# A two-block transformer step on one core: where 72 modulation pieces are reduced, and the order of the first block tile of the second feed-forward layer

## The chip, the cores and the metric

The kernel runs on one core of a Trainium2 chip. The metric is device time in microseconds, the median of the runs of one build. Three runs of the kernel before stand at 2033.03, 2033.26 and 2036.62 us.

## The reference, cut to what matters

Two transformer blocks follow each other on a sequence of 512 positions and width 1024, all in 32-bit floats. The first block has three sublayers: a gated feed-forward layer (`ffn1`), a mixer with a short convolution and stick-breaking attention, and a second gated feed-forward layer (`ffn2`). Each sublayer is modulated by vectors that come from a small input `c`:

```python
c_act = jax.nn.silu(c)
mod = (c_act @ w_ada[l] + b_ada[l]).reshape(B, N_SUBLAYERS, N_MOD, D_MODEL)
u = modulate(rmsnorm(h, norm2_g[l]), mod[:, 1, 0], mod[:, 1, 1])
y = mixer(u, ...)
h = h + mod[:, 1, 2][:, None, :] * y
```

The modulation is one row times a 1024 x 9216 matrix of 36 MB. The second block is not touched by the change.

## The kernel before, in words

Features lie on the 128 partitions, positions on the free axis. Weights come in chunks of 128 x 1024 floats (512 KB). Each chunk is loaded by the SyncE queue (SP) into one of four places of `WRAW` (`Weights.load`, L812), rounded by ScalarE into a high part (`Weights.round`, L823, the instruction is L833) and subtracted by VectorE or GpSimd into a low part (`Weights.low`, L847; `low_pool`, L862). TensorE then multiplies in three passes, high by high, high by low and low by high (`mm3`, L988 to L992). A chunk of 8 slices is 24 matmuls over 512 columns. Four places of high and low parts mean that the rounding of chunk c + 3 waits for the end of chunk c - 1.

Each engine's program is written out by hand, in one order, with semaphores between engines. What stands later in an engine's program waits for what stands before it. SP's queue carries both the weight loads and the loads of the modulation.

**Modulation.** It is cut in 72 pieces, each 128 outputs by 1024 inputs (512 KB). SP loads a piece into a place of `ADA` (`sync_modulation`, L3542, the DMA is L3554), and VectorE multiplies and sums it in one instruction (`dve_modulation`, L2417, the instruction is L2432), then reads the accumulator and, for 40 of the pieces, scales the result. The pieces are counted from 0. Pieces 0 to `ADA_FIRST` - 1 are reduced in the first layer and lie in six places under the arrays `TH1` and `UF1` that the layer forms later; the last of them use only four places. The others are reduced in the mixer and lie in four other places (`ADA1`), which are free once `ffn1` has ended. A load waits for the reduction of the piece that its place held (the fourth before) and of the piece six before.

**The mixer's first 14 chunks** are `mix v` 0 to 3, `mix ga` 0 to 6, `mix q` 0, `mix k` 0 and `mix ga` 7. The four `mix v` chunks all accumulate into four PSUM banks, which VectorE drains at L2677 after the last of them (`v_evac`). There are six banks in the ring, so `mix ga` 0 and 1 go to free banks, and `mix ga` 2 needs the first bank that `v_evac` drains. In VectorE's program of the kernel before, each of the four `mix v` steps has the low part of the chunk three further on and then 4, 3, 3 and 3 pieces; then come the four `v_evac`; then seven `mix ga` steps of a low part and two pieces; then the two last pieces after `qk_evac(0, 0)`. SP loads three pieces beside each `mix v` chunk and two beside the others. The first softmax of the attention (`act_mixer`, the activation at L1959 and its wait ahead of it) waits for the last piece, since its tile `T1` lies over the places of `ADA1`.

**The block tiles of `ffn2`.** From hidden tile 3 on the layer multiplies in seven block products a tile instead of eight (`pe_quads`, L1340). In order of TensorE they are m6, m5, m7, then m1 and m2 of the next tile, then m4 and m3. m1, m6, m7 and m4 accumulate in one bank, and ScalarE takes copies of it in between (`snap`, L2065): m7 waits for the copy after m6, and m4 for the copy after m7. Weight sums `sa` and `sb` are formed by VectorE (`dve_first_sums`, `dve_sums`) and rounded and subtracted like chunks. `c22` is VectorE's sum that m3 waits for. `glu` (`dve_glu`, L2492) is the gated product of hidden tiles 0 to 2, which are made without blocks.

Of the kernel before, what the change touches and what calls it, by code (L numbers as in the profile page):

```python
# [14 lines left out]
KD = D // 128  # L15
# [22 lines left out]
    [(v, m) for v in MOD_ORDER[2:] for m in range(KD)]  # L38
NADA = 6

ADA_FIRST = 43


def ada_place(i):

    if i < ADA_FIRST:
        return 0, i % NADA if i < ADA_FIRST - 4 else i % 4
    return 1, i % 4


# [2003 lines left out]
def act_quads(s, name, p, rest=None):  # L2054


    mem, W, on, act = s.mem, s.W, s.on_act, s.act
    fs, B = QUADS[name][p], mem.blocks[name]
    before = QUADS[name][p - 1][-1] if p and QUADS[name][p - 1] else None
    later = [W.at[name, "down", p, m] for m in range(3)]  # L2060
    M1, U1, U2 = mem.TMP[:, 0, 0:256], mem.TMP[:, 0, 256:S], mem.TMP[:, 1, 0:256]

    def snap(x, f, out):
        on.wait_ge(*s.quad(x, name, f))
        act.activation(out, s.P[:, s.bank[name, "m1", f], 0:256], FN.Copy).then_inc(  # L2065
            *s.snap.inc(x, name, f))

    def silu(f):
        x = B.sil[:, f % 2, :]
        on.wait_ge(*s.comb("c12", name, f))  # L2070
        act.activation(x, x, FN.Silu).then_inc(*s.silu.inc(name, f))

    def upper(f):
        on.wait_ge(*s.glu(name, f))
        if p:
            on.wait_ge(*W.done(W.at[name, "down", p - 1, KD - 1]))
        act.activation(B.hi[:, f - PARTS[p][0], :], B.sil[:, f % 2, :], FN.Copy).then_inc(
            *s.a_hi.inc(name, f))

    if before is not None:  # L2080
        on.wait_ge(*s.comb("c11", name, before))
    snap("m1", fs[0], M1)
    if rest:
        rest()
    W.round(W.gate(name, fs[0] + 1))
    for f in fs:
        W.round(W.up(name, f))
        if f != fs[0]:
            silu(f - 1)
        elif before is not None:  # L2090
            on.wait_ge(*s.comb("c12", name, before))
        snap("m6", f, U1)
        if f != fs[0]:
            upper(f - 1)
        elif before is not None:
            on.wait_ge(*s.glu(name, before))
        if f != fs[-1]:
            W.round(("sb", name, f + 1))
            snap("m7", f, U2)
            W.round(("sa", name, f + 1))  # L2100
            on.wait_ge(*s.comb("c11", name, f))
            snap("m1", f + 1, M1)
            W.round(W.gate(name, f + 2) if f + 2 in fs else later[0])
        else:
            snap("m7", f, U2)
            W.round(later[2])
            silu(f)
            upper(f)
# [380 lines left out]
                      OP.mult).then_inc(*s.fgm.inc())  # L2489


def dve_glu(s, name, e, f, hi, lo, SIL):  # L2492
    dve, on = s.dve, s.on_dve
    if e == "gate":
        return
    x, j = SIL[:, f % 2, :], f - PARTS[PART_OF[f]][0]
    on.wait_ge(*s.W.done(s.W.at[name, "up", f]))
    on.wait_ge(*s.silu(name, f))
    dve.tensor_tensor(x, s.psum(name, "up", f), x, OP.mult).then_inc(*s.glu.inc(name, f))
    on.wait_ge(*s.glu(name, f))  # L2500
    on.wait_ge(*s.a_hi(name, f))
    dve.tensor_tensor(lo[:, j, :], x, hi[:, j, :].bitcast(F32), OP.subtract).then_inc(
        *s.a_lo.inc(name, f))
# [11 lines left out]
def dve_first(s):  # L2515
    mem, W, on, dve = s.mem, s.W, s.on_dve, s.dve

    def down(p, m):
        dve_down(s, "ffn1", p, m, GATE1, s.x_in[m // 2]())
        if p == 2:  # L2520
            dve_total(s, "ffn1", m)

    todo = [(e, f) for f in range(PARTS[0][1]) for e in ("gate", "up")]
    prev = None
    for n, (e, f) in enumerate(todo):
        if n < 5:
            if n == 0:
                W.low(6)
            dve_glu(s, "ffn1", e, f, mem.AH1, mem.AL1, mem.SIL1)
            if n == 4:  # L2530
                dve_modulation(s, 1)
            continue
        if prev:
            dve_glu(s, "ffn1", *prev, mem.AH1, mem.AL1, mem.SIL1)
        W.low(W.at["ffn1", e, f] + 3)
        dve_modulation(s, 2)
        prev = e, f
    dve_glu(s, "ffn1", *prev, mem.AH1, mem.AL1, mem.SIL1)
    assert s.next_ada == ADA_FIRST - 4
    for p in range(3):  # L2540
        if p:
            dve_quads(s, "ffn1", p)
        later = act_later("ffn1", p, W)
        for m in range(KD):
            if m:
                down(p, m - 1)
            if p < 2 and m == 6:
                dve_first_sums(s, "ffn1", PARTS[p + 1][0])
                dve_sums(s, "ffn1", PARTS[p + 1][0])
            W.low(W.at["ffn1", "down", p, m + 3] if m < 5 else later[m - 5])  # L2550
            if p == 0 and m < 4:
                dve_modulation(s, 1)

                x = slice(2 * m, 2 * m + 2)
                on.wait_ge(*s.u_lo_p(2 * m + 1))
                on.wait_ge(*s.u_hi("start", 2 * m + 1))
                dve.tensor_tensor(mem.blocks["ffn1"].full[:, x, :], mem.UH[:, x, :].bitcast(F32),
                                  mem.UL[:, x, :].bitcast(F32), OP.add).then_inc(
                                      *s.comb.inc("u full", m))
                if m == 3:  # L2560
                    on.wait_ge(*s.comb("u full", 3))
                    for t in FORMS:
                        dve_form(s, "ffn1", t)
            if p == 0 and m == 4:
                for t in FORMS:
                    dve_form_low(s, "ffn1", t)
        down(p, KD - 1)
    assert s.next_ada == ADA_FIRST

# [99 lines left out]
def dve_mixer(s):  # L2669
    dve, on, mem, W, Z = s.dve, s.on_dve, s.mem, s.W, s.Z  # L2670
# [9 lines left out]
    def qk_evac(w, p):  # L2680
        dve_pairs(s, "a", w, p, mem.Qa, mem.Ka, mem.KLa,
                  s.psum(("mix q", "mix k")[w], p), 0.125 if w == 0 else 1.0)
# [31 lines left out]

    for q in range(4):
        W.low(W.at["mix v", q] + 3)
        dve_modulation(s, 3 if q else 4)
    for tb in range(4):
        v_evac(tb)
    for m in range(KD - 1):  # L2720
# [4 lines left out]
    dve_modulation(s, 2)  # L2725
    W.low(W.at["mix k", 0] + 3)
    qk_evac(1, 0)
    assert s.next_ada == len(PIECES)
    W.low(W.at["mix ga", KD - 1] + 3)
    on.wait_ge(*s.ple_mm(3))  # L2730
    dve.memset(mem.CV[:, 0:2], 0.0).then_inc(*s.cv.inc("pad"))

# [1 line left out]
    c = W.at["mix ga", KD - 1]  # L2734
# [78 lines left out]
def dve_second(s):  # L2813
    mem, W, on, dve = s.mem, s.W, s.on_dve, s.dve
# [11 lines left out]
        dve_total(s, "ffn2", m, 0)  # L2826
        dve_total(s, "ffn2", m, 1)

    def glu(e, f):
        dve_glu(s, "ffn2", e, f, mem.AH2, mem.AL2, mem.SIL2)  # L2830

    def form(t):
        dve_form_low(s, "ffn2", t)
# [15 lines left out]
    glu("up", 1)  # L2849
    W.low(("sb", "ffn2", 3))  # L2850
    W.low(("sa", "ffn2", 3))
    glu("up", 2)
    for p in range(3):
        dve_quads(s, "ffn2", p)
        later = act_later("ffn2", p, W)
# [755 lines left out]
def sync_mixer(s):  # L3611
# [5 lines left out]
    sync_modulation(s, ADA_FIRST + 3)  # L3617
    for c in range(W.at["mix v", 0], W.at["mix ga", KD - 1] + 1):
        W.load(c + 7)
        sync_modulation(s, s.ada_at + (2 if c < W.at["mix ga", 0] else 1))  # L3620
    assert s.ada_at == len(PIECES)

    def gb_out(m):
# [269 lines left out]
```

## Time and profile before

| what | value |
|---|---|
| median of three runs | 2033.26 us |
| the profiled execution, its own time | 2033.56 us |
| its span, first to last instruction | 2032.3 us |
| TensorE busy | 1995.2 us, 98% of the span |
| VectorE busy | 1287.0 us, 63% |
| ScalarE busy | 929.9 us, 46% |
| GpSimd busy | 291.7 us, 14% |
| mean granted TensorE clock | 0.998 |

The table is of one profiled execution. Matmuls are pipelined, so a duration of a matmul (0.39 us for 512 columns) is longer than the distance between two starts; the distance is what a matmul costs. The times of the rows further down count from the first instruction. A row of the timeline gives start, duration, engine, line, operation and tiles, and in brackets the idle time of that engine just before and what ended it.

### The profile page before, as it was taken

To read this page: it belongs to the slowest core of one execution; us is meant where nothing else is said; L and a number is where in the kernel's file an instruction comes from. 1 tells how busy PE (TensorE), PEld (TensorE's weight loads), DVE (VectorE), ACT (ScalarE), POOL (GpSimd) and SP (SyncE) were. 2 spreads that over 40 slices of the span, in tenths; PEclk is the share of its full clock that TensorE was granted. 3 is DMA by queue.
4 is the path that set the end of the run, shared out by engine and by line. 5 is a ranking of instruction groups with operands and counts; after the bars stand their busy time and mean duration, and the time that the engine had idled before them with its cause. 6 is when DMAs were issued, how large, how long until landed. Compare 5 with 4: busy or idle time off the path is not lost.

```text
span 2032.3 us, 27032 instructions
## 1 busy us (share of the span) xinstructions
PE 1995.2 (98%) x10637; PEld 1726.1 (85%) x10637; DVE 1287.0 (63%) x1915; ACT 929.9 (46%) x1356; POOL 291.7 (14%) x219
## 2 busy tenths in 40 slices
PE   6999999989999999999999999999999999999998
PEld 5889999778888889899898888888888888888888
DVE  6888767685565668577576445454376575563666
ACT  4334525425656545345255455554434343342444
POOL 5000000002101200000000344443000021020130
PEclk9999999999999999999999999999999999999999
DMA  8943424692223533323233433333535333333232
GB/s 307 334 140 99 123 79 118 216 339 76 77 83 104 181 99 108 116 84 115 84 106 122 131 119 104 119 102 123 196 106 170 99 109 100 94 99 98 82 113 76
DMA packets 84398, 261.49 MB, mean 129 GB/s; under 512 B 9248, under 2 KB 13472, under 8 KB 84272
## 3 DMA queue, kind: packets, MB, share of 16 engines
q1 hardware_dynamic: 84272, 259.77, 39.8%
q8 instruction: 84, 1.38, 0.3%
q14 instruction: 42, 0.34, 0.1%
HBM read 242.92 MB, written 16.81 MB: 128 GB/s over the span
## 4 chain that ended last, share of the span: by engine, by line
PE 72%; DVE 4%; ACT 3%; issue 1%; DMA 1%; POOL 0%; DVEq 0%; SPq 0%; ACTq 0%
PE P L990 22%; PE P L991 22%; PE P L992 22%; PE P L1225 1%; PE P L1507 1%; DMA ADA<-w_ada 1%; PE P L1237 1%; PE P L1236 1%; ACT WH L833 1%; DVE WL L847 0%; DVE ADA L2432 0%; PE P L1554 0%; DVE SL L2754 0%; DVE TMP L2610 0%; ACT UH L2317 0%
## 5 line engine op out<-in xcount | busy, mean ns | idle before, releaser
L990 PE MATMUL P<-UH,WH 128*128 128x512 f32 (+1 forms) x1563 | 581.5, 372 | 11.8 <-DVE V L2677 5.2
L991 PE MATMUL P<-UL,WH 128*128 128x512 f32 (+1 forms) x1563 | 577.1, 369 | 0.0
L992 PE MATMUL P<-UH,WL 128*128 128x512 f32 (+1 forms) x1563 | 577.1, 369 | 0.0
L833 ACT ACTIVATE WH<-WRAW 128x1024 fp32r<-128x1024 f32 (+2 forms) x311 | 311.2, 1011 | 437.5 <-PE P L992 433.9
L847 DVE TENSOR_TENSOR WL<-WRAW,WH 128x1024 fp32r<-128x1024 f32 (+2 forms) x252 | 303.1, 1206 | 76.7 <-ACT WH L833 76.1
L990 PEld LDWEIGHTS P<-UH,WH 128*128 128x128 f32 x1563 | 295.9, 189 | 61.8 <-issue 10.9
L992 PEld LDWEIGHTS P<-UH,WL 128*128 128x128 f32 x1563 | 295.8, 189 | 49.9
L991 PEld LDWEIGHTS P<-UL,WH 128*128 128x128 f32 x1563 | 296.1, 189 | 47.3
L862 POOL TENSOR_TENSOR WL<-WRAW,WH 128x1024 fp32r<-128x1024 f32 x59 | 144.7, 2454 | 356.8 <-ACT WH L833 356.8
L990 PE MATMUL P<-AH,WH 128*128 128x512 f32 x478 | 186.6, 390 | 0.0
L991 PE MATMUL P<-AL,WH 128*128 128x512 f32 x478 | 186.1, 389 | 0.0
L992 PE MATMUL P<-AH,WL 128*128 128x512 f32 x478 | 186.0, 389 | 0.0
L992 PEld LDWEIGHTS P<-AH,WL 128*128 128x128 f32 x478 | 89.7, 188 | 18.8
L990 PEld LDWEIGHTS P<-AH,WH 128*128 128x128 f32 x478 | 89.8, 188 | 18.6 <-POOL AL L3510 0.4
L991 PEld LDWEIGHTS P<-AL,WH 128*128 128x128 f32 x478 | 89.8, 188 | 18.1
L990 PE MATMUL P<-TH,WH 128*128 128x256 f32 x352 | 99.7, 283 | 0.7 <-ACT TMP L2065 0.7
L992 PE MATMUL P<-TH,WL 128*128 128x256 f32 x352 | 99.6, 283 | 0.0
L991 PE MATMUL P<-TL,WH 128*128 128x256 f32 x352 | 99.6, 283 | 0.0
L3401 POOL TENSOR_TENSOR R<-VAR,NEGHALF 128x4 f32<-128x4 f32 (+1 forms) x9 | 10.4, 1157 | 607.7 <-DVE VAR L2982 362.7
L2432 DVE CUSTOM_DVE_ANT_0 ADA<-ADA,CB,COLS 128x1024 f32<-128x1024 f32 x56 | 75.4, 1352 | 8.3 <-DMA ADA<-w_ada 8.2
L2511 DVE SCALAR_TENSOR_TENSOR H<-P,MOD,H 128x512 f32<-128x512 f32 x48 | 35.9, 748 | 67.7 <-PE P L992 67.7
L3278 DVE SCALAR_TENSOR_TENSOR Y<-ZP,COLS,Y 128x512 f32<-128x512 f32 x88 | 69.1, 785 | 14.5 <-ACT Y L2296 12.8
(347 smaller groups left out, 3564.9 us busy)
## 6 DMA issues: line engine op xcount, KB each, us to landing
WRAW<-w_gu SPq DMA_DIRECT2D x88, 512.0 KB, 3.6
ADA<-w_ada SPq DMA_DIRECT2D x72, 512.0 KB, 5.9
WRAW<-w_down SPq DMA_DIRECT2D x48, 512.0 KB, 3.6
WRAW<-w_up SPq DMA_DIRECT2D x44, 512.0 KB, 3.6
WRAW<-w_in SPq DMA_DIRECT2D x40, 512.0 KB, 3.6
WRAW<-w_mix SPq DMA_DIRECT2D x36, 512.0 KB, 3.6
WRAW<-w_down SPq DMA_DIRECT2D x24, 384.0 KB, 3.1
WRAW<-w_out SPq DMA_DIRECT2D x16, 512.0 KB, 4.1
```

Source lines behind the costliest of these rows:

```text
L833: s.act.activation(hi, self.raw(item), FN.Copy).then_inc(*self.rounded.inc(item))
L847: s.dve.tensor_tensor(lo, self.raw(item), hi.bitcast(F32), OP.subtract).then_inc(*self.low_v.inc(item))
L862: s.pool.tensor_tensor(lo, self.raw(item), hi.bitcast(F32), OP.subtract).then_inc(*self.low_p.inc(item))
L990: pe.matmul(out, wh, xh, start=start, stop=False, skip_group_check=True)
L991: pe.matmul(out, wh, xl, start=False, stop=False, skip_group_check=True)
L992: return pe.matmul(out, wl, xh, start=False, stop=stop, skip_group_check=True)
L1225: s.pe.matmul(out, x, y, start=start and i == 0, stop=False, skip_group_check=True)
L1236: pe.matmul(ob[:, 128 * j:S], v, hi[:, of], start=j == 0, stop=False, skip_group_check=True)
L1237: last = pe.matmul(ob[:, 128 * j:S], v, lo[:, of], start=False, stop=j == 3, skip_group_check=True)
L2432: dve.tensor_tensor_reduce(piece, piece, c, 1.0, s.col("b_ada", v * KD + m), OP.mult, OP.add, mod).then_inc(*s.ada.inc(i, "sum"))
L2511: s.dve.scalar_tensor_tensor(h, s.psum(name, "down", p, m), s.mod(gate, m), h, OP.mult, OP.add).then_inc(*s.resid.inc(name, p, m))
L3278: dve.scalar_tensor_tensor(y, mem.ZP[:, n % 3, j:S + j], s.col("conv_w_2", 2 * NF * j + i), y, OP.mult, OP.add).then_inc(*s.conv.inc(e, f, j))
```

## The change

Four edits go together for the modulation. `ADA_FIRST` goes from 43 to 44, so one more piece is reduced in `ffn1`, in the step of the first `down` chunk (two pieces there, one in each of the next three). In the mixer VectorE reduces two pieces in each of fourteen steps: the four `mix v` steps, the seven `mix ga` steps, and after `qk_evac(0, 0)`, after `qk_evac(1, 0)` and after the low part three chunks past `mix ga` 7. That is 8 + 14 + 2 + 2 + 2 = 28. SP loads two pieces beside each chunk instead of three beside the first four. Its four pieces ahead of the first stay.

In `ffn2`, ScalarE rounds the gate chunk of hidden tile 4 before it makes the high part of `glu` 2 instead of after it, and VectorE subtracts that chunk's low part between the product of `glu` 2 and its low part. In the first block tile (hidden tile 3) the copies after m7 and after m1 of the next tile go ahead of the rounding of both weight sums.

```diff
-ADA_FIRST = 43
+ADA_FIRST = 44
@@ ada_place
-        return 0, i % NADA if i < ADA_FIRST - 4 else i % 4
+        return 0, i % NADA if i < ADA_FIRST - 5 else i % 4
@@ act_quads
     snap("m1", fs[0], M1)
+    W.round(W.gate(name, fs[0] + 1))
     if rest:
         rest()
-    W.round(W.gate(name, fs[0] + 1))
...
         if f != fs[-1]:
-            W.round(("sb", name, f + 1))
-            snap("m7", f, U2)
-            W.round(("sa", name, f + 1))
-            on.wait_ge(*s.comb("c11", name, f))
-            snap("m1", f + 1, M1)
+            if rest and f == fs[0]:
+                snap("m7", f, U2)
+                on.wait_ge(*s.comb("c11", name, f))
+                snap("m1", f + 1, M1)
+                W.round(("sa", name, f + 1))
+            else:
+                W.round(("sb", name, f + 1))
+                snap("m7", f, U2)
+                W.round(("sa", name, f + 1))
+                on.wait_ge(*s.comb("c11", name, f))
+                snap("m1", f + 1, M1)
@@ dve_glu
     dve.tensor_tensor(x, s.psum(name, "up", f), x, OP.mult).then_inc(*s.glu.inc(name, f))
+    if rest:
+        rest()
@@ dve_first
-                dve_modulation(s, 1)
+                dve_modulation(s, 1 if m else 2)
@@ dve_mixer
     for q in range(4):
         W.low(W.at["mix v", q] + 3)
-        dve_modulation(s, 3 if q else 4)
+        dve_modulation(s, 2)
...
     W.low(W.at["mix k", 0] + 3)
     qk_evac(1, 0)
+    dve_modulation(s, 2)
+    W.low(W.at["mix ga", KD - 1] + 3)
+    dve_modulation(s, 2)
     assert s.next_ada == len(PIECES)
-    W.low(W.at["mix ga", KD - 1] + 3)
@@ dve_second
-    glu("up", 2)
+    glu("up", 2, lambda: W.low(W.gate("ffn2", 4)))
@@ sync_mixer
         W.load(c + 7)
-        sync_modulation(s, s.ada_at + (2 if c < W.at["mix ga", 0] else 1))
+        sync_modulation(s, s.ada_at + 1)
```

`W.round(("sa", ...))` works through the list of preparations up to its item, and `sb` stands before `sa` in it, so both are rounded there.

## Rows read from the trace of the kernel before

**Rows 1.** Waits of TensorE: total us, times, longest.
```profile
PE P L990 <- DVE V L2677: 5.2, 1, 5.2
PE P L990 <- DVE WL L847: 1.2, 1, 1.2
```

**Rows 2.** Busy time by window: us, then each engine, clock, DMA share, GB/s.
```profile
400.00:405.00 5.00, 3.94 (x18) 2.94 (x16) 3.68 (x7) 0.96 (x1) 0.00 (x0) 1.00 1.03 411
...
421.50:425.00 3.50, 3.40 (x8) 2.75 (x9) 3.50 (x5) 0.00 (x0) 0.00 (x0) 0.51 0.63 249
```

**Rows 3.** Timeline of ScalarE, the roundings that wait for a chunk's end.
```profile
404.04 1.06 ACT L833 ACTIVATE WH<-WRAW 128x1024 fp32r<-128x1024 f32 x1 [4.10 <-PE P L992]
410.97 1.06 ACT L833 ACTIVATE WH<-WRAW 128x1024 fp32r<-128x1024 f32 x1 [3.92 <-PE P L992]
...
429.00 1.06 ACT L833 ACTIVATE WH<-WRAW 128x1024 fp32r<-128x1024 f32 x1 [10.91 <-PE P L992]
...
434.44 1.06 ACT L833 ACTIVATE WH<-WRAW 128x1024 fp32r<-128x1024 f32 x1 [3.80 <-PE P L992]
```

**Rows 4.** Timeline of VectorE from the first mixer piece to the V drain.
```profile
397.44 1.29 DVE L2432 CUSTOM_DVE_ANT_0 ADA<-ADA,CB,COLS 128x1024 f32<-128x1024 f32 x1 [3.53 <-DMA ADA<-w_ada]
...
401.37 1.29 DVE L2432 CUSTOM_DVE_ANT_0 ADA<-ADA,CB,COLS 128x1024 f32<-128x1024 f32 x1 [1.32 <-DMA ADA<-w_ada]
...
403.86 1.22 DVE L847 TENSOR_TENSOR WL<-WRAW,WH 128x1024 fp32r<-128x1024 f32 x1
...
410.50 1.28 DVE L2432 CUSTOM_DVE_ANT_0 ADA<-ADA,CB,COLS 128x1024 f32<-128x1024 f32 x1
...
415.25 1.22 DVE L847 TENSOR_TENSOR WL<-WRAW,WH 128x1024 fp32r<-128x1024 f32 x1
...
420.77 2.48 DVE L2677 TENSOR_TENSOR V<-P,V 128x512 fp32r<-128x512 f32 x4
```

**Rows 5.** Timeline of SP, the first mixer pieces issued.
```profile
393.60 1.80 SPq L3554 DMA_DIRECT2D ADA<-w_ada  x4
...
398.77 4.26 SPq L3554 DMA_DIRECT2D ADA<-w_ada  x3
```

**Rows 6.** Tile ADA, 393 to 465 us.
```profile
DMA to landing us min/median/max: 3.8/5.8/7.7
```

**Rows 7.** Timelines of VectorE and ScalarE, head 0.
```profile
465.17 1.39 DVE L2651 TENSOR_TENSOR aKL<-P,aK 64x512 fp32r<-64x512 f32 x2 [1.34 <-ACT aK L1854]
...
476.87 2.08 DVE L2754 TENSOR_TENSOR SL<-T,SH 128x1280 fp32r<-128x1280 f32 x1 [1.52 <-ACT SH L1966]
...
469.99 1.23 ACT L1959 ACTIVATE T<-P 128x1280 f32<-128x1280 f32 x1
```

**Rows 8.** Chain of waits, TensorE's first use of the softmax.
```profile
484.85 1.23 PE P L1294 x8
```

**Rows 9.** Timeline of TensorE, first block tile of `ffn2`.
```profile
786.67 0.28 PE L991 MATMUL P<-TL,XH 128*128 128x256 f32 x1
786.79 0.28 PE L992 MATMUL P<-TH,XL 128*128 128x256 f32 x1
787.42 0.39 PE L990 MATMUL P<-TH,XH 128*128 128x256 f32 x1 [0.35 <-ACT TMP L2065]
...
792.73 0.39 PE L990 MATMUL P<-TH,WH 128*128 128x256 f32 x1 [0.73 <-ACT TMP L2065]
```

**Rows 10.** Timelines of ScalarE and VectorE, the same tile.
```profile
785.53 1.05 ACT L833 ACTIVATE XH<-WRAW 128x1024 fp32r<-128x1024 f32 x1
...
791.34 1.06 ACT L833 ACTIVATE WH<-SB 128x1024 fp32r<-128x1024 f32 x1 [3.98 <-DVE SB L2894]
...
793.58 0.42 DVE L2919 TENSOR_TENSOR TMP<-P,TMP 128x256 f32<-128x256 f32 x1
```

**Rows 11.** Timelines of VectorE and TensorE, before `ffn1`'s first block tile.
```profile
140.97 4.62 DVE L2585 TENSOR_TENSOR TL<-UF,TH 128x1024 fp32r<-128x1024 f32 x4
...
156.50 0.28 PE L990 MATMUL P<-UH,WXH 128*128 128x256 f32 x1
```

More of the change, by code:

```diff
@@ L2489, in dve_start, with dve_glu @@
                       OP.mult).then_inc(*s.fgm.inc())
-def dve_glu(s, name, e, f, hi, lo, SIL):
+def dve_glu(s, name, e, f, hi, lo, SIL, rest=None):
     dve, on = s.dve, s.on_dve
@@ L2538, in dve_first @@
     dve_glu(s, "ffn1", *prev, mem.AH1, mem.AL1, mem.SIL1)
-    assert s.next_ada == ADA_FIRST - 4
+    assert s.next_ada == ADA_FIRST - 5
     for p in range(3):
@@ L2827, in down, with glu @@
         dve_total(s, "ffn2", m, 1)
-    def glu(e, f):
-        dve_glu(s, "ffn2", e, f, mem.AH2, mem.AL2, mem.SIL2)
+    def glu(e, f, rest=None):
+        dve_glu(s, "ffn2", e, f, mem.AH2, mem.AL2, mem.SIL2, rest)
     def form(t):
```

## The prediction

> **What bounds the kernel now.** The first view to read is the waits of TensorE, since that engine is busy 98% of the span and has only a handful of idle places left. Two of them lie in the mixer's first chunks and both name VectorE [rows 1]: 5.2 us before `mix ga` 2, which waits for the V drain, and 1.2 us before `mix ga` 0, which waits for its low part. VectorE is busy 63% over the whole span, so its mean says nothing here. Its own timeline does [rows 4]: the low part of `mix ga` 0 stands behind four pieces and starts at 403.86, and the V drain stands behind thirteen pieces and starts at 420.77. The pieces in turn came late because SP could issue the first only at 393.60 [rows 5] and the DMA engines were full from 400 on, at 411 GB/s [rows 2]. So this stretch is bounded by loading and reducing pieces ahead of two things that TensorE needs, while the places where the pieces are needed themselves are far away.
>
> The second view is the window after the gap: in 421.5 to 425 the granted clock is 0.51, the lower of its two levels (1.2 instead of 2.4 GHz), right after TensorE had stood still for over 5 us; in the windows before it it is 1.00 [rows 2]. The gap costs twice.
>
> What both cost together is read from ScalarE, whose roundings start as a chunk ends [rows 3]. Undisturbed, 429.00 to 434.44 is 5.44 us a chunk. The end of `mix v` 3 is at 404.04, those of `mix ga` 0 and 2 at 410.97 and 429.00.
>
> **The mixer, what can be won.** From 404.04 to 429.00 are 24.96 us for three chunks, which at 5.44 need 16.32. Lost: 24.96 - 16.32 = 8.64 us. It splits as 6.93 - 5.44 = 1.49 for the low part and 18.03 - 10.88 = 7.15 for the V drain with the slow clock. The ceiling of this part is 8.6 us; by TensorE's own starts the idle stretches and half of the slow window of 3.5 us [rows 2] come to a little less, so I take 8.5.
>
> **The mixer, replayed.** A piece costs VectorE 1.28 us [rows 4], or 1.45 with its scaling as I take it, a low part 1.15 to 1.22. TensorE ends `mix v` 3 at about 403.8, and then wants `mix ga` 0 at 403.8, `mix ga` 1 at 409.2, `mix ga` 2 at 414.7.
> - Step 0 has two pieces. They land as now, so they run from 397.44 to about 400.0. The low part of `mix ga` 0 follows and ends at 401.3, where it now starts at 403.86. Wanted at 403.8: 2.5 us to spare, the gap of 1.2 goes.
> - Step 1: the third piece can start at 401.37, as now, when it lands [rows 4]; the two end at 403.9, the low part of `mix ga` 1 at 405.1. Wanted at 409.2.
> - Step 2: these pieces are issued when the first two places come free, at 398.77 [rows 5] and about 400.1. With the median of 5.8 us to landing [rows 6] they are there at 404.6 and 405.9; reduced by 407.8, and the low part of `mix ga` 2 ends at 409.0, where it now starts at 415.25. Wanted at 414.7.
> - Step 3: issued at about 402.6 and 403.9, landed at 408.4 and 409.7, or with the longest landing of 7.7 us [rows 6] the last at 411.6. Reduced by 411.8 (412.9 at the longest). The V drain starts then; TensorE started 421.60 - 420.77 = 0.83 us after the drain's start [rows 4, 1], so the bank is free at 412.7 (413.8). Wanted at 414.7: 2.0 us to spare (0.9).
>
> A check from the other side, without any thought on the DMA: even if nothing landed earlier than now, the eighth piece starts at 410.50 [rows 4]. One low part more ahead of it makes that 411.7, the piece ends at 413.0 and the bank is free at 413.9, still before 414.7. So the gap before `mix ga` 2 goes whole and so does the slow clock behind it. The bounds of this part are 8.6 us won, and 3.9 us won if the last piece came 3 us too late and the clock fell again (8.6 - 3.0 - 1.7); I take 8.5, since both replays end there.
>
> After that a step of VectorE is two pieces and a low part, 2.6 to 2.9 + 1.2 = 3.8 to 4.1 us, in a chunk of 5.44. Loads: three times 524 KB in 5.44 us is 289 GB/s, against the 411 seen [rows 2]. Nothing builds up.
>
> On that the Trainium skill, "DMA: Bandwidth & Descriptors", section "Where 436 GB/s comes from", speaks against me: it says that loads from HBM are held to about 358 GB/s for a core. The trace exceeds it, with 411 over 5 us [rows 2]. By 411 the eleven transfers up to the eighth piece (5.77 MB) take 14.0 us, by 358 they take 16.1; as an estimate from that page, the rule would take 2.1 us of step 3's spare time, leave nothing of it, and by it the rival of a rest of the gap would be about twice as likely as I put it below.
>
> **What is moved, and who waits for it.** (a) Pieces at the tail. VectorE now does its last four pieces, in two pairs, after `qk_evac(1, 0)`, which ends at 466.6 now [rows 7] and at 458.1 when all is 8.5 us earlier. Four pieces with scaling, 4 x 1.39 = 5.6 us, end at about 463.6. The first softmax activation, now at 469.99 [rows 7], would start at 461.5 and waits 2.1 us for the last piece. Behind it in ScalarE's program stand the rest of head 0's softmax and the roundings. TensorE fills with three chunks and wants the result at 484.69 to 484.85 [rows 8]; VectorE delivers it at 476.87 + 2.08 = 478.95 [rows 7]. Of 5.7 us spare 2.1 are used. Cost 0; if the cover were gone it would be the 2.1. (b) SP: fewer pieces stand ahead of the weight loads in the first steps, so these go out earlier; at the tail the load behind the last two pieces waits for a low part that comes after their places are free. Cost 0: a load is issued for the chunk seven further on, 38 us at 5.44 a chunk. (c) The piece in `ffn1` costs VectorE 1.3 us in the first `down` step, and its load holds the next weight load by about 1.5 us. The forms behind it end at 140.97 + 4.62 = 145.6, and TensorE's first block matmul is at 156.50 [rows 11]: 10.9 us spare. Cost 0, and at most 0 gained, as TensorE isn't idle there.
>
> **The block tile.** Matmuls over 256 columns start 0.12 us apart (786.67, 786.79). 786.79 to 787.42 is 0.63, so 0.51 is lost before m7; before m4 the same reading of the idle 0.73 gives 0.90 [rows 9]. Ceiling 1.41. The copy that m7 waits for stands behind the rounding of the gate chunk at 785.53 [rows 10], 0.95 us at ScalarE's pace; moved into ScalarE's idle time before the `glu` product, it lets the copy run at 786.05, before m5 has ended at 786.9. The first 0.51 goes. The copy that m4 waits for stands behind the rounding of `sb`, which waits 3.98 us for VectorE's sum [rows 10]; ahead of it, it runs at about 788.5, and m4 starts when m2 ends, at 791.3. The next late thing is `c22`, which m3 waits for: it stands in VectorE's program behind the low part of `sb`, and its rounding starts with the sum, 1.1 us earlier than now because VectorE's work moved up by that. `c22`, now 793.58 to 794.0 [rows 10], ends at 792.9, and m3 is wanted at 792.7. So 0.25 stays: 1.15 won. Bounds: 1.41 won, and 0.74 lost, if `sb` were late for m6 by the two copies (0.37 each) now ahead of it. I take 1.15, as m6 of tile 4 is wanted at 794.5 and the low part is there at 792.5.
>
> **Sum.** 8.5 + 1.15 = 9.65 us. Between 830 and 1970 us TensorE never waits, and the head gaps of the mixer hang on chains that move with it, so nothing takes it back. The profiled execution took 2033.56, 1.26 more than its span; it becomes 2023.9. The median is 0.3 lower: 2033.26 - 9.65 = 2023.6.
>
> **Rivals.**
> - A rest of the gap stays before `mix ga` 2, because the extra weight loads now share the DMA engines with the pieces. For it: 411 GB/s is all that they gave [rows 2], and a landing of 7.7 us has been seen [rows 6]. Against it: the check above. At 3 us of idle time and a slow clock after it, 8.5 - 4.7 + 1.15 = 4.95 won: 2028.3. Chance 0.10.
> - The block tile gives nothing, `c22` or `sb` taking the place of the copies: 2033.26 - 8.5 = 2024.8; at its worst bound 2025.5. For it: VectorE is all but busy there. Chance 0.10.
> - The gain is given back later in the mixer, no change: 2033. Against it: no idle time of TensorE outside the head gaps. Chance 0.04.
> - Slower: the last piece holds head 0. Place: the first softmax activation, its price one for one in TensorE from the point where the last piece ends 3.6 us after 463.6, that is after 467.2. To be slower than before it must end after 467.2 + 9.65 = 476.9; at 481 the time would be 2037.4. For it: the two last pieces are issued only when the pair before the last is reduced, behind a weight load that waits for GpSimd. Against it: they are issued at about 453 and land by 461 even at 7.7 us. Chance 0.02.
> - The forecast: 0.74.
>
> **How the numbers follow.** The likeliest is 2023.6, with its own range of 2022.4 to 2025. The range for 8 in 10 takes in the second rival and the mild form of the first: 2021.5 to 2026.8. A measurement of this kernel tells about 0.2%, 4.1 us, from no change. Faster by more: 0.74 + 0.10 + 0.10 less a little for a first rival in its worst form, 0.93. Within it 0.05, slower 0.02.
>
> **What would show it.** No wait of TensorE at the V drain and none at `mix ga` 0's low part; roundings of ScalarE from 404.04 on every 5.44 us; clock 1.00 through 425; the V drain starting between 411 and 414; the first softmax activation waiting for a piece by about 2 us and TensorE not waiting at L1294 in head 0; in `ffn2` m7 without a wait and at most 0.3 us left at m3. Wrong would be: a V drain after 414.7, or a wait of TensorE in head 0 that is not in the list now.

## The result and the profile after

The changed kernel takes 2023.26 us, the median of four runs (2023.12 to 2023.8), beside 2033.28 for the kernel before (2033.03 to 2036.62, four runs). The ratio is 0.9947, with a 95% interval of 0.993 to 0.9965: 0.35 to 0.7% faster. The median fell by 10.0 us, forecast were 9.65. The profiled execution took 2023.12, with a span of 2021.9 and a mean granted clock of 0.998.

The waits of TensorE after, where those of [rows 1] stood; columns: engine, tile, line, released by, total us, times, longest:

```profile
PE P L1303 <- DVE RL L2775: 2.7, 4, 0.8
PE P L1294 <- DVE SL L2765: 0.7, 2, 0.3
PE P L990 <- DVE TMP L2930: 0.2, 1, 0.2
```

Neither the V drain nor the low part of `mix ga` 0 is in the list any more. Of `ffn2`'s first block tile 0.2 is left, at m3. The first two lines are head gaps of the mixer, which were there before.

Busy time by window after (us, then each engine, granted clock, DMA share, GB/s). The first window is the full load of [rows 2] seen about two microseconds earlier, the others are the places of the gap and of the lower clock:

```profile
398.00:403.00 5.00, 5.00 (x24) 4.14 (x23) 3.93 (x6) 0.90 (x2) 0.00 (x0) 1.00 1.03 410
416.40:421.50 5.10, 5.10 (x24) 4.24 (x23) 4.99 (x11) 1.64 (x2) 0.00 (x0) 1.00 0.93 304
421.50:425.00 3.50, 3.50 (x17) 2.88 (x16) 3.46 (x7) 0.26 (x1) 0.00 (x0) 1.00 0.92 303
```

TensorE is busy in all of it, and from 421.5 to 425 it is granted 1.00 where it had 0.51. ScalarE's roundings, which start as a chunk ends, answer to [rows 3]:

```profile
402.98 1.06 ACT L833 ACTIVATE WH<-WRAW 128x1024 fp32r<-128x1024 f32 x1 [4.10 <-PE P L992]
408.42 1.06 ACT L833 ACTIVATE WH<-WRAW 128x1024 fp32r<-128x1024 f32 x1 [2.44 <-PE P L992]
413.86 1.06 ACT L833 ACTIVATE WH<-WRAW 128x1024 fp32r<-128x1024 f32 x1 [2.37 <-PE P L992]
419.30 1.06 ACT L833 ACTIVATE WH<-WRAW 128x1024 fp32r<-128x1024 f32 x1 [3.80 <-PE P L992]
```

Three chunks take 419.30 - 402.98 = 16.32 us, to the hundredth the undisturbed pace, where they took 24.96.

VectorE after, from the first mixer piece to the V drain, answers to [rows 4]:

```profile
396.38 1.28 DVE L2438 CUSTOM_DVE_ANT_0 ADA<-ADA,CB,COLS 128x1024 f32<-128x1024 f32 x1 [3.51 <-DMA ADA<-w_ada]
...
399.07 1.28 DVE L2438 CUSTOM_DVE_ANT_0 ADA<-ADA,CB,COLS 128x1024 f32<-128x1024 f32 x1 [1.40 <-DMA ADA<-w_ada]
400.28 1.22 DVE L847 TENSOR_TENSOR WL<-WRAW,WH 128x1024 fp32r<-128x1024 f32 x1
...
410.45 1.27 DVE L2438 CUSTOM_DVE_ANT_0 ADA<-ADA,CB,COLS 128x1024 f32<-128x1024 f32 x1
411.90 2.47 DVE L2686 TENSOR_TENSOR V<-P,V 128x512 fp32r<-128x512 f32 x4
```

The low part of `mix ga` 0 now starts at 400.28 (before at 403.86), the V drain at 411.90 (before at 420.77).

Where the 10.44 us between the two profiled executions lie (2033.56 - 2023.12):

| stretch | before | after | difference |
|---|---|---|---|
| span's start to the start of `mix v` 0 | 381.90 | 380.87 | -1.0 |
| from there to head 0's scores | 84.92 | 76.25 | -8.7 |
| `ffn2`, first block tile, 97 starts of matmuls | 13.11 | 11.97 | -1.1 |
| everything else | | | +0.4 |

The third row counts from the first to the last of 97 starts of matmuls. That is 96 distances, and without a stop they take 96 x 0.12 = 11.52 us.

The first row is not the change's work: TensorE's granted clock comes up for good at 29.0 us in the one execution and at 26.7 in the other, and in the twelve further traces at 24.7 to 29.2. Of the last row 0.5 stands at the very end: the clock falls to its lower level 8.6 us before the span's end, 6.5 before.

### The profile page after: what moved, and what is told of

Its sections match the earlier page's. It is cut to its first block, busy times and chain, and to the rows that moved or that the text cites. A ratio compares the mean times of both kernels' runs of the same rounds, so it can differ in the third digit from the quotient of the medians.

```text
span 2021.9 us, 27033 instructions
## 1 busy us (share of the span) xinstructions
PE 1992.1 (99%) x10637; PEld 1724.7 (85%) x10637; DVE 1283.2 (63%) x1915; ACT 930.0 (46%) x1356; POOL 292.2 (14%) x219
## 4 chain that ended last, share of the span: by engine, by line
PE 93%; DVE 3%; ACT 3%; issue 1%; DMA 0%; POOL 0%; SPq 0%; DVEq 0%; ACTq 0%; POOLq 0%
PE P L990 29%; PE P L992 29%; PE P L991 29%; PE P L1225 1%; PE P L1507 1%; PE P L1237 1%; PE P L1236 1%; ACT WH L833 0%; PE P L1103 0%; DVE SQ L2419 0%; PE P L1554 0%; DVE WL L847 0%; DVE SL L2765 0%; DMA H<-x 0%; ACT UH L2323 0%
## 5 line engine op out<-in xcount | busy, mean ns | idle before, releaser
L833 ACT ACTIVATE WH<-WRAW 128x1024 fp32r<-128x1024 f32 (+2 forms) x311 | 311.2, 1011 | 424.1 <-PE P L992 420.4
L3412 POOL TENSOR_TENSOR R<-VAR,NEGHALF 128x4 f32<-128x4 f32 (+1 forms) x9 | 10.4, 1157 | 605.8 <-DVE VAR L2993 361.6
L3289 DVE SCALAR_TENSOR_TENSOR Y<-ZP,COLS,Y 128x512 f32<-128x512 f32 x88 | 69.1, 785 | 14.5 <-ACT Y L2302 12.8
```

The source lines that it names most:

```text
L833: s.act.activation(hi, self.raw(item), FN.Copy).then_inc(*self.rounded.inc(item))
L3289: dve.scalar_tensor_tensor(y, mem.ZP[:, n % 3, j:S + j], s.col("conv_w_2", 2 * NF * j + i), y, OP.mult, OP.add).then_inc(*s.conv.inc(e, f, j))
```

## The experiments

Each line of a diff is against the changed kernel. The differences are taken against the kernel before in the same comparison; its median was 2033.7 to 2034.6 there.

### The parts alone

The mixer's and first layer's part alone; all edits in `ffn2` undone (`act_quads` goes back to its old order as well):

```
-    glu("up", 2, lambda: W.low(W.gate("ffn2", 4)))
+    glu("up", 2)
```

> The modulation's part of the change alone; the block tile of ffn2 stays as before. Theory (the two parts add up, each where the prediction put it): TensorE has no wait at the V drain or at mix ga 0's low part, the two waits of 0.35 and 0.73 us in ffn2's first block tile are back, and the time is 1.1 us over the changed kernel's 2023.3: 2024.4, some 8.8 below before. Rival (the mixer gives less than its 8.6 and the rest of the 10.0 came from the start of the run, where the clock rose 2.3 us earlier in the one trace): that part stays a matter of each run, and the medians would give 7.5 to 8.2 below before, 2025.1 to 2025.8.

Measured: 2024.47 us (2024.05 to 2026.18), ratio 0.9954 (0.9942 to 0.9967), 9.7 us faster where I had 8.8: the time is the expected one, the kernel before was slower in this comparison. The stretch from `mix v` 0 to the scores is 76.26 long, as in the changed kernel, and the two waits of [rows 9] are back, 0.35 and 0.73, with 13.11 us for the 97 starts.

The tile alone; the modulation's spread undone, with the last two pairs at the end taken out, the other counts and SP's as before:

```
-ADA_FIRST = 44
+ADA_FIRST = 43
-        dve_modulation(s, 2)
+        dve_modulation(s, 3 if q else 4)
```

> The order of ffn2's first block tile alone; the modulation as before. Theory: 1.15 us off the path, 2032.1, both waits of TensorE at the copies gone and 0.2 to 0.3 us at m3 in their place. Rival (the copies' waits are only moved on, c22 or sb taking their place): no wait less in sum, 2033.2. The gaps of 1.2 and 5.2 us in the mixer stay as they were in either case.

Measured: 2032.71 us (2030.54 to 2034.8), ratio 0.9994 (0.9985 to 1.0003), 1.5 us faster by the medians; the interval holds no change. By the trace the tile is 11.97 long, as in the changed kernel. Its wait at the V drain, and the window behind it:

```profile
PE P L990 <- DVE V L2686: 6.1, 1, 6.1
```
```profile
421.50:427.00 5.50, 5.50 (x14) 4.30 (x15) 5.50 (x9) 0.00 (x0) 0.00 (x0) 0.53 0.71 249
```

The same program of modulation as before, yet a gap of 6.1 instead of 5.2, and behind it TensorE works 5.3 us at the lower clock instead of 3.4. So this stretch isn't the same in every execution. That fits how far apart the runs lie: those of the kernel before 3.6 to 5.1 us in each comparison (2030.9 to 2035.7 here), those of the changed kernel, where the stretch is gone, 0.7, though the mixer's part alone, without the gap as well, has 2.1. The parts add up: 9.7 + 1.1 by the trace are 10.8, and the changed kernel's 2023.3 lies 10.9 below this comparison's 2034.2.

### Inside the mixer's part

SP's loads as before, three pieces for each step of `mix v`:

```
-        sync_modulation(s, s.ada_at + 1)
+        sync_modulation(s, s.ada_at + (2 if c < W.at["mix ga", 0] else 1))
```

> The changed kernel, but SP loads three pieces beside each mix v chunk as before, so that only VectorE's order is new. Theory (what freed TensorE is VectorE's order, not thinner loading): 2023.3, no wait at the V drain; weight loads go out behind one piece more each, with a lead of seven chunks that is not used up. Rival (three pieces and a weight in 5.44 us, 386 GB/s, fill the DMA engines, so the pieces that count come later): the V drain starts 1.5 to 3 us later than in the changed kernel and TensorE waits 0.5 to 2 us before mix ga 2: 2024 to 2027.

Measured: 2023.34 us (2022.72 to 2023.81), ratio 0.9946 (0.9933 to 0.996). The V drain starts at 410.1, 1.8 earlier than in the changed kernel's trace, and buys nothing, for there TensorE didn't wait. Nor is the 1.8 the work of these loads: the next run has the changed kernel's loads up to the drain, and there it starts at 410.0. SP's edit by itself is worth nothing here.

One piece less in the first layer, three at the very end, and SP issues one more beside `mix ga` 0:

```
-ADA_FIRST = 44
+ADA_FIRST = 43
-                dve_modulation(s, 1 if m else 2)
+                dve_modulation(s, 1)
-    dve_modulation(s, 2)
+    dve_modulation(s, 3)      # the last of the three calls
```

> The changed kernel with ADA_FIRST 43 again: the 29th piece is reduced at the very end, three after mix ga 7's low part. Theory (the 44th piece in ffn1 only keeps the tail short, and the tail has spare time): the first softmax activation waits about 1.4 us longer for the last piece than in the changed kernel (3.5 instead of 2.1), TensorE still doesn't wait in head 0, 2023.3. Rival (the tail is on the path): 1.4 us more, 2024.7.

Measured: 2023.02 us (2022.31 to 2023.84), ratio 0.9945 (0.9931 to 0.9958). The first softmax activation, by ScalarE's timeline (in brackets what it waited and for whom):

```profile
463.38 1.24 ACT L1959 ACTIVATE T<-P 128x1280 f32<-128x1280 f32 x1 [3.44 <-DVE MOD L2438]
```

It waits 3.44 us, and TensorE none: that wait has cover. The 44th piece in the first layer costs and brings nothing.

Eight pieces at the tail, none beside the last two `mix ga` steps of the loop:

```
-        dve_modulation(s, 2)
+        dve_modulation(s, 2 if m < 5 else 0)
...
-    dve_modulation(s, 2)
+    dve_modulation(s, 4)      # both of the last two calls
```

> The changed kernel with no pieces in the steps of mix ga 5 and 6, and four instead of two in each of the last two places, so that eight pieces stand behind qk_evac(1, 0). Theory (head 0 has 3.9 us to spare in the changed kernel, 471.07 to 474.91): there are four places, so the fifth to eighth of the tail can be loaded only as the first four are reduced, 5 to 6 us each from issue to landing; the last ends 7.5 us later than now, the first softmax activation waits some 9.5 us, and TensorE waits 2 to 4.5 us at L1294 in head 0: 2025.3 to 2028. This is the mechanism of the slower rival of the prediction, forced. Rival (head 0 has fill enough, the softmax is not near the path): no wait, 2023.2.

Measured: 2029.79 us (2029.01 to 2030.84), ratio 0.9979 (0.997 to 0.9989). TensorE's waits, ScalarE's timeline, and the window behind the wait:

```profile
PE P L1294 <- DVE SL L2765: 4.7, 3, 4.1
```
```profile
470.43 1.25 ACT L1959 ACTIVATE T<-P 128x1280 f32<-128x1280 f32 x1 [10.22 <-DVE MOD L2438]
```
```profile
479.00:484.00 5.00, 4.94 (x17) 4.56 (x18) 3.71 (x7) 4.14 (x6) 1.47 (x1) 0.50 0.25 92
```

The place of the slower rival is real: where the activation waits 10.22 us, 4.1 reach TensorE, within my 2 to 4.5. But the clock is at 0.50 for 6.8 us, from 477.4 on. TensorE starts again at 479.1 and works the last 5.2 of them at half speed, of which half, 2.6, is lost as well. 4.1 + 2.6 = 6.7 explains the excess over the changed kernel, 6.5; without the clock my 2025.3 to 2028 was too low.

### How thick the pieces may stand

Three pieces in the first two steps, two in the last two, one pair less at the end:

```
-        dve_modulation(s, 2)
+        dve_modulation(s, 3 if q < 2 else 2)
```

> The changed kernel with 3, 3, 2 and 2 pieces in VectorE's four mix v steps instead of 2 each; the last pair of the tail goes instead. Theory (the replay: each piece ahead of the V drain is 1.4 us, and the drain has about 1 us to spare at TensorE): in the changed kernel's trace the drain starts 8.9 us after mix v 3's end, in others of its kind 7.5; two pieces more make 11.7 or 10.3, with 0.83 to the first matmul 12.5 or 11.1, against the 10.88 of two chunks. TensorE waits 0.2 to 1.7 us before mix ga 2 and the clock stays up: 2023.5 to 2025. Rival (loading and not VectorE's queue sets the drain, e3's loads showing that there is room): the two pieces hide in waits and nothing is lost, 2023.2.

Measured: 2032.46 us (2030.67 to 2035.0), ratio 0.9993 (0.9983 to 1.0002). Missed: I had 2023.5 to 2025, and nothing of the mixer's gain is left. TensorE's waits:

```profile
PE P L990 <- DVE V L2686: 3.8, 1, 3.8
...
PE P L1225 <- DVE aKL L2660: 1.7, 1, 1.7
```

Three pieces in all four steps, two pairs less at the end:

```
-        dve_modulation(s, 2)
+        dve_modulation(s, 3)
```

> The same with 3 pieces in each of the four mix v steps, 12 ahead of the drain (13 in the kernel before, 8 in the changed one). Theory: four pieces more are 5.6 us, so the drain starts 13.1 to 14.5 us after mix v 3's end and TensorE waits 3.0 to 4.5 us before mix ga 2; the low part of mix ga 0 behind three pieces comes 0 to 0.3 us late. If the clock falls after it as it did after 5.2 us, 1.7 to 3.4 us more: 2026.3 to 2027.9 without, 2028 to 2031 with. Rival (the gain came from thinner loading in the four steps): SP loads as in the changed kernel, so no more than 1 us is lost.

Measured: 2060.8 us (2060.15 to 2062.44), ratio 1.0131 (1.0115 to 1.0148): 27 us slower than before, far outside what I expected. Its waits:

```profile
PE P L990 <- DVE V L2686: 12.1, 1, 12.1
PE P L1225 <- DVE aKL L2660: 9.3, 1, 9.3
PE P L990 <- DVE WL L847: 7.7, 4, 3.1
```

My replays had counted VectorE's work and the DMA engines' rate. Neither is full here: VectorE waits 43.6 us for pieces, in 16 places. VectorE's timeline and SP's queue in the same stretch:

```profile
426.50 1.22 DVE L847 TENSOR_TENSOR WL<-WRAW,WH 128x1024 fp32r<-128x1024 f32 x1
...
432.61 1.28 DVE L2438 CUSTOM_DVE_ANT_0 ADA<-ADA,CB,COLS 128x1024 f32<-128x1024 f32 x1 [4.90 <-DMA ADA<-w_ada]
```
```profile
427.74 0.33 SPq L821 DMA_DIRECT2D WRAW<-w_mix  x1
428.11 0.91 SPq L3563 DMA_DIRECT2D ADA<-w_ada  x2
```

The low part ends at 427.72. At 427.74 SP issues the weight load, whose place that low part has freed, and only behind it, at 428.11, the two pieces that VectorE wants next; they need 4.5 us to land, and VectorE waits 4.90. VectorE is busy 38.5 of the 73 us from 393 to 466, and the DMA engines' share is 0.59. The places of the two pieces had long been free: the pieces that they held before, the ninth and the tenth, were reduced by 417.5. What held them is SP's program: they stand behind a load that waits for the step in which they are needed.

That can be counted. Four pieces are issued before step 0, and `sync_modulation` adds two at a step (three with the old count), then comes the weight load that waits for the step's low part. The lead of step j is the number of pieces issued ahead of that load, less the number that VectorE needs up to the end of the step. The waits are those from 393 us to head 0's scores; 3.4 to 3.5 us of each is the wait for the first piece:

| version | needed to steps 0..3 | issued ahead | lead | VectorE waits for pieces | V drain starts |
|---|---|---|---|---|---|
| before | 4, 7, 10, 13 | 4, 7, 10, 13 | 0, 0, 0, 0 | 8.2 (8 times) | 420.8 |
| changed | 2, 4, 6, 8 | 4, 6, 8, 10 | 2, 2, 2, 2 | 4.9 (2) | 411.9 |
| 2 a step, old loads | 2, 4, 6, 8 | 4, 7, 10, 13 | 2, 3, 4, 5 | 3.7 (2) | 410.1 |
| 3, 3, 2, 2 | 3, 6, 8, 10 | 4, 6, 8, 10 | 1, 0, 0, 0 | 14.5 (11) | 417.5 |
| 3 a step | 3, 6, 9, 12 | 4, 6, 8, 10 | 1, 0, -1, -2 | 43.6 (16) | 424.1 |

Below zero a piece can't land before the step's own low part; at zero it may be issued in time but has no cushion. The count was made after these results, so it needed a test: the same two versions with the old loads, which lift the lead and change nothing else.

```
-        dve_modulation(s, 2)
+        dve_modulation(s, 3)
...
-        sync_modulation(s, s.ada_at + 1)
+        sync_modulation(s, s.ada_at + (2 if c < W.at["mix ga", 0] else 1))
```

> As the run with 3 pieces in each of the four mix v steps (which lost 37 us), but SP loads three pieces beside each mix v chunk, as before the change. New theory (that run lost its time because a step needed pieces whose loads stood in SP's queue behind a weight load that waits for the same step's low part: by step j it needs 3j + 3 pieces and only 4 + 2j are issued ahead of that load; with three beside each chunk 4 + 3j are): the loss of 37 falls to what queue and places cost. With four places the twelfth piece ends two landings and a half after the fourth, at about 417.1 on the changed kernel's scale, and TensorE waits 3 to 4.5 us before mix ga 2, plus 1.7 to 3.4 for the clock: 2027.5 to 2031, and no wait at the later mix ga chunks. Rival (the reductions' number alone did it): 2055 to 2061 again.

Measured: 2030.77 us (2029.5 to 2031.88), ratio 0.9981 (0.9971 to 0.999), as expected. Thirty of the 37.5 us that three a step had cost are back by one line in SP's program, which makes the leads 1, 1, 1, 1. VectorE waits 7.4 (4 times) instead of 43.6, and of TensorE's later waits 0.2 is left. What remains, a little more than the 3 to 4.5 that I had:

```profile
PE P L990 <- DVE V L2686: 4.8, 1, 4.8
```

This part is VectorE's work: twelve pieces and four low parts ahead of the drain, which starts at 418.7. From the second piece, at 399.86, up to it VectorE stands still for 0.05 us in all.

```
-        dve_modulation(s, 2)
+        dve_modulation(s, 3 if q < 2 else 2)
...
-        sync_modulation(s, s.ada_at + 1)
+        sync_modulation(s, s.ada_at + (2 if c < W.at["mix ga", 0] else 1))
```

> As the run with 3, 3, 2 and 2 pieces (2032.5), but SP loads three beside each mix v chunk. New theory: the tenth piece ends at 413.7 or so on the changed kernel's scale, TensorE waits 0.3 to 1.7 us before mix ga 2 instead of 3.8, the clock stays up, the wait of 1.7 us at head 0's scores goes: 2023.5 to 2025.5. Rival (lead of the loads is not it): 2032 again.

Measured: 2027.62 us (2027.01 to 2027.86), ratio 0.9965 (0.9952 to 0.9979). The drain starts at 415.7 instead of 417.5, the wait at the scores is gone, VectorE waits 5.8 (4 times) instead of 14.5: the count, by which the leads are now 1, 1, 2, 3, holds. The time is 2 us above my range. The wait, and the window behind it:

```profile
PE P L990 <- DVE V L2686: 1.9, 1, 1.9
```
```profile
416.50:420.00 3.50, 3.47 (x9) 2.77 (x10) 3.50 (x5) 0.00 (x0) 0.00 (x0) 0.55 0.88 304
```

I had expected a gap of 0.3 to 1.7 and a clock that stays up. It was 1.9, and the clock was 0.55 over 3.5 us behind it.

### Inside the block tile

The gate chunk's move alone, with the copies in the old order:

```
-            if rest and f == fs[0]:
-                snap("m7", f, U2)
-                on.wait_ge(*s.comb("c11", name, f))
-                snap("m1", f + 1, M1)
-                W.round(("sa", name, f + 1))
-            else:
```

> The changed kernel with the copies after m7 and m1 behind the roundings of the weight sums again, so that of the block tile's part only the gate chunk's earlier preparation is left. Theory (the two waits are two causes): the wait of 0.35 us at m7 stays gone, the wait of 0.73 at m4 is back at 0.4 to 0.9 us, nothing at m3; 0.5 to 0.9 us over the changed kernel in the trace from 742 us on. Rival (one cause): both waits stay away, or both are back.

Measured, one run: 2022.56 us. The 97 starts take 11.89 us, so it holds 1.22 of the 13.11. I had expected the tile 0.5 to 0.9 slower than in the changed kernel; it is 0.08 faster. One stop is there, at m4, 0.38 by the starts, and m3's is gone. ScalarE's timeline:

```profile
779.91 1.06 ACT L833 ACTIVATE WH<-SB 128x1024 fp32r<-128x1024 f32 x1 [3.72 <-DVE SB L2899]
780.88 0.36 ACT L2065 ACTIVATE TMP<-P 128x256 f32<-128x256 f32 x1
```

The copies' move alone, with the gate chunk in its old place:

```
-    W.round(W.gate(name, fs[0] + 1))      # ahead of the glu product
+    W.round(W.gate(name, fs[0] + 1))      # behind it, as before
-    glu("up", 2, lambda: W.low(W.gate("ffn2", 4)))
+    glu("up", 2)
```

> The changed kernel with the gate chunk prepared after glu 2's high part again, so that of the block tile's part only the copies' move is left. Theory: the wait of 0.35 us at m7 is back, the one at m4 stays gone and what is left at m3 is the same 0.2 us or more, since VectorE's work is not moved up any more: c22 comes 1.1 us later against a TensorE that is 0.5 later, so 0.7 to 0.9 us at m3. Rival: as for the run beside it.

Measured, one run: 2024.72 us, of which the tile is 12.91, so this move alone holds 0.20. TensorE's timeline, m7 and then m3:

```profile
777.28 0.39 PE L990 MATMUL P<-TH,XH 128*128 128x256 f32 x1 [0.28 <-ACT TMP L2065]
...
783.90 0.38 PE L990 MATMUL P<-UH,WH 128*128 128x256 f32 x1 [0.60 <-DVE TMP L2930]
```

m3's wait is there, 0.60 where I had expected 0.7 to 0.9: what one saves at m4 comes back at the next matmul, while VectorE's sums stand where they stood.

### A version from both findings

`c22` ahead of the low part of `sb` in the first tile of `ffn2`, and one pair of pieces moved from the very end to before `qk_evac(0, 0)`, where VectorE has room:

```
+    dve_modulation(s, 2)
     qk_evac(0, 0)
     dve_modulation(s, 2)
...
     W.low(W.at["mix ga", KD - 1] + 3)
-    dve_modulation(s, 2)
...
+            if (name, f) == ("ffn2", 3):
+                c22(f)
+                W.low(("sb", name, f + 1))
```

> Two edits to the changed kernel: in ffn2's first block tile VectorE does c22 ahead of the low part of sb, and in the mixer's tail the pair after qk_evac(0, 0) goes ahead of it, into the 7 us in which VectorE stands still there, and so do the two pairs behind it, so that nothing is left after mix ga 7's low part. Theory: the 0.2 us wait at m3 (0.36 by the starts) goes, the 2.06 us wait of the first softmax activation goes and brings TensorE nothing, since it did not wait there: 0.36 less, 2022.9, not to be told from 2023.2 by time, but by the two waits. Rival (ScalarE's 2 us in head 0 are felt later, in the waits of 0.3 and 0.8 us of the following heads): these shrink as well and 1 us or more is won.

Measured: 2022.33 us (2022.25 to 2022.93), ratio 0.994 (0.9926 to 0.9955). The 97 starts take 11.52, the wait at m3 is gone, and the activation waits for nothing:

```profile
460.37 1.23 ACT L1959 ACTIVATE T<-P 128x1280 f32<-128x1280 f32 x1
```

It is 0.9 us below the changed kernel by the medians, and its trace says 0.45 of it is the tile; the rest is less than can be told, as is the 0.9 itself. Moving the pieces away from head 0 gives nothing, since the wait there was covered.

## Why the prediction was right, point by point

**The mixer, 8.5 forecast.** Right: 8.67 from `mix v` 0 to the scores, 8.64 by ScalarE's roundings, which is the whole ceiling. Both costs went together, the idle time and the lower clock behind it. The mixer's part alone keeps it, the tile alone has none of it.

**Two steps of the replay.** The low part of `mix ga` 0 was forecast to end at 401.3 and ended at 401.50. The V drain was forecast at 411.8, with 2.0 us spare, or 0.9 at the longest landing. It started at 411.90. But the whole timeline had moved 1.0 to the left, so both were a microsecond late, and that the numbers meet is luck. TensorE began `mix ga` 2 at 413.60, and 413.60 - 411.90 - 0.83 = 0.87 us were spare. In six other kernels whose pieces up to the drain stand as here it was 1.1 to 2.3.

The forecast had the landings of steps 2 and 3 as what sets the drain. The trace after shows another cause. VectorE waited 1.40 us for the second piece, at 399.07, which I had taken to follow the first without a wait, and from there to the drain it never stood still: no piece of steps 1 to 3 was waited for, and the rest is VectorE's own work. The six others agree. With waits of 1.34 and 1.07 for the second piece the spare time was 1.1 and 1.4; in the four where it was 0.3 or less it was 1.8 to 2.3. What the replay lacked is how far the second piece's landing varies, 4.6 to 6.1 us from its issue in these seven traces.

The check from the other side, by which nothing could be late enough, held, though its margin of 0.8 was thinner than the forecast let it seem: 3, 3, 2, 2 has only two pieces more ahead of the drain, and it lost everything.

**The DMA engines' rate.** I kept the trace's 411 GB/s against the 358 of the Trainium skill, "DMA: Bandwidth & Descriptors", section "Where 436 GB/s comes from". The trace after has 410 over 398 to 403, so here too the measurement decides against the page. The 2.1 us that the rule would have taken from step 3 were not taken; since no piece of step 3 was waited for, a somewhat slower rate need not have shown in the time either.

**Head 0.** Forecast: the activation waits 2.1 us for the last piece, and TensorE doesn't. The rows of after, ScalarE's, VectorE's and the chain's:

```profile
462.44 1.25 ACT L1959 ACTIVATE T<-P 128x1280 f32<-128x1280 f32 x1 [2.06 <-DVE MOD L2438]
```
```profile
469.23 1.84 DVE L2765 TENSOR_TENSOR SL<-T,SH 128x1280 fp32r<-128x1280 f32 x1 [1.41 <-ACT SH L1966]
```
```profile
475.15 1.23 PE P L1294 x8
```

2.06 measured. The product ends at 471.07, TensorE uses it from 475.15: 4.1 us of cover are left where I had 3.6. The versions with waits of 3.44 and 10.22 bracket the point from which the place decides: at 3.44 nothing reaches TensorE, at 10.22 4.1 do, so, one for one, it lies near 6.1.

**The block tile, 1.15 forecast.** The total is right, 13.11 - 11.97 = 1.14. Two sizes behind it were not, and they cancel: the start after each stop comes 0.10 late as well, so by the starts the two stops cost 1.6 and not 1.41, and 0.46 and not 0.25 is left at m3 (0.20 of it idle, on `TMP` from VectorE). The attribution was wrong, too. I had booked 0.51 on the gate chunk's move and 0.64 on the copies' move. Alone they give 1.22 and 0.20, and on top of the gate's move the copies' move costs 0.08 (11.89 to 11.97). The step that failed is "the copy that m4 waits for stands behind the rounding of `sb`, which waits 3.98 us": true of before, but the gate chunk's low part, too, leaves its place in front of VectorE's sums, those come some 1.2 us earlier, and `sb`'s rounding and the copy behind it with them. I had used that time for `c22` and not for the copy. And the copies' move has a price: with them ahead of it `sb`'s rounding starts at 780.56, 0.25 after its sum has ended, which puts off the low part of `sb` and `c22` behind it, so the stop saved at m4 (0.38) comes back at m3 (0.46).

**What was not forecast.** The start of the run, 1.0 us of the difference between the profiled executions, is the clock's and goes both ways. The end gave 0.5 back by the clock. The two parts of the forecast are 8.67 + 1.14 = 9.8 us by the traces. That the medians differ by nearly the same, 10.0, is in part luck, since the start, the end and the gap each move by more than the rest. And the gap of the kernel before isn't the same each time, as the tile alone shows; its medians in the later comparisons are 2033.7 to 2034.6. Against these the changed kernel's 2023.3 would be 10.4 to 11.3 us faster. The 9.65 was right for the execution it was made from.

**The rivals.** "A rest of the gap" is what 3, 3, 2, 2 with the old loads is, and at 2027.62 it came near the 2028.3 that I had worked out from 3 us of gap; the gap was 1.9. "The last piece holds head 0" exists as a mechanism, 4 us of wait beyond where the changed kernel stands.

## What to carry to other kernels

When loads of two kinds are issued from one queue in program order, count for each step how many of the one kind stand ahead of the first load that waits for that step, and subtract what the step needs; here at a lead of one or more nearly all of the transfers hide, at zero the cushion is gone, and below zero every step pays a landing (2060.8 against 2030.8 us by one line), though neither the DMA engines nor VectorE are full. A short wait of TensorE is to be priced with the clock behind it, which here cost 1.7 to 3.0 us on top of idle times of 1.9 us and more. And when two edits stand in one tile, the one that moves the producer's sums forward may already free the waits that the other was meant for: time each alone.

## What the runs showed of the chip

The granted clock fell to the lower of its two levels (1.2 of 2.4 GHz) behind idle times of TensorE much shorter than the 5.2 us of before, and neither that nor how long it stayed there followed the idle time alone. The table has every idle time above 1.5 us after the first 30 us that began at the upper level:

| kernel | TensorE idle, us | at the lower level, us | of these with TensorE at work, us |
|---|---|---|---|
| 3, 3, 2, 2 | 1.7 (at the scores) | none | |
| 3, 3, 2, 2, old loads | 1.9 | 3.4 | 3.4 |
| 3 a step | 2.5 | none | |
| 3 a step | 3.1 | 3.4 | 3.4 |
| 3, 3, 2, 2 | 3.8 | 6.8 | 5.7 |
| eight at the tail | 4.1 | 6.8 | 5.2 |
| 3 a step, old loads | 4.8 | 6.8 | 4.7 |
| before | 5.2 | 3.4 | 3.4 |
| tile alone | 6.1 | 6.8 | 5.3 |
| 3 a step | 9.3 | 10.2 | 4.3 |
| 3 a step | 12.1 | 13.7 | 6.0 |

In six of the nine falls the clock was down 1 us or more before TensorE started again. For 3, 3, 2, 2, busy time by window, the idle part and the part at work:

```profile
417.19:418.30 1.11, 0.00 (x1) 0.03 (x1) 1.07 (x5) 0.00 (x0) 0.00 (x0) 0.50 1.01 399
418.30:424.02 5.72, 5.72 (x14) 4.48 (x15) 5.65 (x11) 0.00 (x0) 0.00 (x0) 0.50 0.40 132
```

A lower clock costs only while TensorE works, so half of the last column is lost on top of the idle time: 1.7 us for the kernel before, 1.7 to 3.0 in the others. None of the idle times of 0.2 to 1.0 us in the block tile or the heads was followed by a fall. The idle time alone decides neither whether the clock falls, with none after 2.5 us and one after 1.9, nor for how long. What does isn't settled by these runs.

A second thing: a piece, else 1.28 us, took 3.42 us on VectorE at 441.22 in the kernel before, beside a low part of 2.54 us that GpSimd began at 441.02, and another took 3.16 at 452.22, beside one of 2.40 from 451.90. In the changed kernel it happens once; timelines of VectorE and GpSimd:

```profile
431.80 3.41 DVE L2438 CUSTOM_DVE_ANT_0 ADA<-ADA,CB,COLS 128x1024 f32<-128x1024 f32 x1
```
```profile
431.32 2.81 POOL L862 TENSOR_TENSOR WL<-WRAW,WH 128x1024 fp32r<-128x1024 f32 x1 [37.84 <-ACT WH L833]
```

In all three the piece starts while GpSimd's low part runs, and ends 1.08 us after it (435.21 and 434.13 here). A piece that starts first keeps its 1.28: the one at 430.59, for instance. And in the first layer a piece of the other form, with an operand `P` from PSUM in place of `CB`, isn't slowed:

```profile
23.65 1.27 DVE L2438 CUSTOM_DVE_ANT_0 ADA<-ADA,P,COLS 128x1024 f32<-128x1024 f32 x1
```
```profile
22.78 2.39 POOL L862 TENSOR_TENSOR WL<-WRAW,WH 128x1024 fp32r<-128x1024 f32 x1
```

The slow pieces lie where VectorE has room. A plan that lets a piece of the mixer's form start behind a low part of GpSimd would have to reckon with up to 2.1 us for it.
